# Window attention scores: 64 query rows as they lie in two array halves, no spread copy, blocks written out, the scaling ahead of the next maximum

## The chip, the cores and the metric

The kernel runs on one core of one Trainium2 chip. Its time is the device time of one execution in microseconds (us). The profile is one more execution, recorded by the hardware profiler.

## The reference, cut to what matters

One inference step of a hybrid decoder with two layers, for 1024 prompt tokens and 8 single sample tokens. Each layer projects its input, runs an RWKV-7 time mixing on 8 heads and a sliding-window attention with sinks on 8 query heads (4 to each of 2 key/value heads), then an output projection and a SwiGLU network. The change touches the prompt's attention alone:

```python
def swa_banded(q, k, v, sink):            # T = 1024, BLOCK = WINDOW = 128, HEAD_DIM = 64
    nb = T // BLOCK                       # 8 blocks
    ...
    s = jnp.einsum('bnqkgd,bnskd->bnkgqs', qb, kb).astype(F32) * ATTN_SCALE   # 128 queries x 256 keys
    mask = ((diff >= 0) & (diff < WINDOW))[None] & (kpos >= 0)[:, None, :]
    p = sink_softmax(s, mask, sink[None, None, :, :, None, None])
    o = jnp.einsum('bnkgqs,bnskd->bnqkgd', p.astype(vb.dtype), vb)

def sink_softmax(s, mask, sink):
    s = jnp.where(mask, s, -jnp.inf)
    m = jnp.maximum(jnp.max(s, axis=-1, keepdims=True), sink)
    p = jnp.exp(s - m)
    return p / (jnp.sum(p, axis=-1, keepdims=True) + jnp.exp(sink - m))
```

## The kernel before, in words

Everything lies transposed: 128 rows of features, tokens along the free axis. `proj[:, 15:19]` holds the rotated queries, two heads of 64 rows to a plane, and `kd[:, g]` holds key head g twice, in rows 0 to 63 and in rows 64 to 127. The engines follow programs written by hand, one for each (`block.sync`, `block.gpsimd`, `block.scalar`, `block.vector`, `block.tensor`), and meet by semaphores alone. A layer is a sequence of stages: the input projection, rotation of q and k, the prompt's attention, the sample tokens' attention, the RWKV part, the output projection, the feed-forward part. The stage of the change starts when the last rotated key is there (`kd_last`) and ends when the last block's output has been split (`low`, line 1109); the sample tokens' attention waits for that (line 1724).

In this stage each engine calls its own `blocks(n, q, S, M, V)` for n from -1 to 8. Three parts of three different query blocks stand in one call: S makes the scores of block n+1, M the softmax of block n, V the output of block n-1. The calls for n from 1 to 6 are a hardware loop of three rounds with two calls in each; the others are written out. The parts in one call:

- ScalarE (lines 646 to 686): **bdq**, two copies that put the queries of block n+1 into `q_spread`, where each head's 64 rows have their own 128 columns and the other 64 rows are zero; **vp** and **ptc1**, evictions of transposed values and probabilities; 8 exponentials (`exp0` to `exp7`) that start with a wait for `negmax` of block n, with **ptc3** between the fourth and the fifth; `sinkexp`; `vblk`; **high**, the rounded half of the output of block n-1, which waits for its matmuls `pv`; the scaling of heads 5 to 7.
- VectorE (lines 1061 to 1110): **ptc0**; **sc0** to **sc3**, which take the scores out of banks 0 to 3 with scale and mask, with **ptc2** behind sc0; the **maximum** over 8 heads and three small operations to `negmax` (block n+1); `den` and `recip`, which wait for `sinkexp` (block n); the **scaling** of heads 0 to 4; **low**.
- TensorE (lines 1653 to 1714): `vt`; the transposes **pt0** and **pt1** of the probabilities of block n-1, which wait for both engines' scaling; the scores of the first head pair (**s0**); **pt2** and **pt3**, where pt2 waits for ptc0 and pt3 for ptc1, as they reuse banks 4 and 5; the scores of the other three pairs; the 16 matmuls **pv**, which wait for ptc2 and ptc3.

The scores are computed with all 128 rows, 8 matmuls of 256 columns for a block:

```python
last = mm(bank[p][:, 256 * h:256 * h + 256], bdq[:, p, 128 * h:128 * h + 128],
          kd[:, p // 2, bass.ds((n + 1) * WIN, 2 * WIN)], start=True, stop=True)
```

A float32 matmul stands as two MATMUL records in the trace. sc0 of block n+1 waits for pt3 of block n-1 as well, since both use one score tile.

## Time and profile before

| | |
|---|---|
| three runs, median (lowest to highest) | 3289.95 us (3284.81 to 3290.27) |
| the profiled execution's own time | 3289.88 us |
| its span, first to last instruction | 3287.9 us |
| mean granted TensorE clock | 0.93 |
| busy: TensorE, VectorE, ScalarE, GpSimd | 90%, 45%, 26%, 19% |
| DMA | 158.04 MB, 48 GB/s |

The profile counts from the first instruction. PE is TensorE's matmuls, PEld its weight loads, DVE VectorE, ACT ScalarE. A row of a timeline gives start, length, engine, line, operation, output and inputs, how many of a kind were merged, and in brackets the idle time ahead and who ended it. The stage of the change takes 310.9 to 424.3 in the first layer and about 1935.4 to 2049.1 in the second; the span outside these stretches is some 3060 us.

### The profile page before, as it was taken

What the parts mean: (1) busy time and instruction counts of PE and PEld (TensorE: products, weight loads), DVE (VectorE), ACT (ScalarE), POOL (GpSimd) and SP (SyncE); (2) the same over time, 40 slices, a digit from 0 to 9 for tenths busy, and PEclk for the clock granted to TensorE, in tenths of its full rate; (3) what the DMA queues carried; (4) which work ended last, traced back from release to release, by engine and by line L of the source; (5) the groups of instructions that cost most, each with busy time, mean ns of one, the idle gap of its engine ahead of it and who ended that gap; (6) DMA issues with size and microseconds to landing.
All of it is one profiled execution on the core that took longest, in us unless ns stands there. A gap on an engine that the chain in (4) does not pass through costs nothing.

```text
span 3287.9 us, 49756 instructions
## 1 busy us (share of the span) xinstructions
PE 2954.0 (90%) x20858; PEld 2779.5 (85%) x20858; DVE 1464.9 (45%) x2549; ACT 840.2 (26%) x1759; POOL 609.1 (19%) x297
## 2 busy tenths in 40 slices
PE   6996866997899999999999968579898999999997
PEld 6995745886899999999999947368788999999997
DVE  5335638766632232222363265497646232222324
ACT  3001633341321111111321025424424111111112
POOL 2320001002322212222123100010133212222123
PEclk9998876898999999999999988669899999999998
DMA  3101010003211111111221010100222111111111
GB/s 118 47 32 51 1 39 7 18 19 130 86 46 45 51 41 52 46 46 49 69 71 45 20 52 0 39 11 15 97 80 71 47 45 52 46 45 46 45 52 52
DMA packets 55875, 158.04 MB, mean 48 GB/s; under 512 B 9200, under 2 KB 23536, under 8 KB 54896
## 3 DMA queue, kind: packets, MB, share of 16 engines
q1 hardware_dynamic: 52496, 150.76, 14.2%
q0 software_dynamic: 3168, 4.23, 0.5%
q8 instruction: 162, 2.65, 0.3%
q14 instruction: 49, 0.40, 0.0%
HBM read 137.43 MB, written 17.54 MB: 47 GB/s over the span
## 4 chain that ended last, share of the span: by engine, by line
PE 76%; DVE 13%; issue 5%; ACT 4%; DMA 1%; POOL 0%; SPq 0%; DVEq 0%; ACTq 0%; POOLq 0%
PE bank L1606 20%; PE bank L1608 20%; PE bank L1607 20%; PE bank L1681 2%; PE bank L1713 2%; PE bank L1674 1%; PE bank L1974 1%; PE bank L1970 1%; PE bank L1831 1%; PE bank L1950 1%; PE bank L1773 1%; PE bank L1865 1%; PE bank L1960 1%; DVE c_T L1226 1%; DVE c_NT L1224 1%
## 5 line engine op out<-in xcount | busy, mean ns | idle before, releaser
L1606 PE MATMUL bank<-act_high,w_high 128*128 128x344 f32 x3504 | 1138.1, 325 | 50.8 <-POOL w_low L491 35.6
L1608 PE MATMUL bank<-act_high,w_low 128*128 128x344 f32 x3504 | 1128.5, 322 | 0.0
L1607 PE MATMUL bank<-act_low,w_high 128*128 128x344 f32 x3504 | 1128.2, 322 | 0.0
L491 POOL TENSOR_TENSOR w_low<-w_raw,w_high 128x1024 fp32r<-128x1024 f32 x206 | 521.9, 2539 | 1678.5 <-ACT w_high L580 1661.5
L1606 PEld LDWEIGHTS bank<-act_high,w_high 128*128 128x128 f32 x3504 | 667.8, 191 | 59.6 <-POOL w_low L491 40.4
L1607 PEld LDWEIGHTS bank<-act_low,w_high 128*128 128x128 f32 x3504 | 666.6, 190 | 2.4 <-issue 1.7
L1608 PEld LDWEIGHTS bank<-act_high,w_low 128*128 128x128 f32 x3504 | 667.2, 190 | 0.0
L1469 DVE TENSOR_TENSOR f_mid<-f_silu,bank 128x344 f32<-128x344 f32 x132 | 67.7, 513 | 852.9 <-PE bank L1608 849.7
L1566 DVE TENSOR_TENSOR resid<-bank,resid 128x344 f32<-128x344 f32 x528 | 270.4, 516 | 209.8 <-PE bank L1608 209.8
L1606 PE MATMUL bank<-f_mid_high,w_high 128*128 128x344 f32 x1056 | 341.3, 323 | 4.1 <-DVE resid L1566 4.0
L1608 PE MATMUL bank<-f_mid_high,w_low 128*128 128x344 f32 x1056 | 339.2, 321 | 0.0
L580 ACT CAST w_high<-w_raw 128x1024 fp32r<-128x1024 f32 x206 | 212.5, 1043 | 490.2 <-PE bank L1608 487.1
L1607 PE MATMUL bank<-f_mid_low,w_high 128*128 128x344 f32 x1056 | 337.0, 319 | 0.0
L1606 PEld LDWEIGHTS bank<-f_mid_high,w_high 128*128 128x128 f32 x1056 | 198.1, 188 | 10.7 <-DVE resid L1566 10.1
L1608 PEld LDWEIGHTS bank<-f_mid_high,w_low 128*128 128x128 f32 x1056 | 198.7, 188 | 0.0
L1607 PEld LDWEIGHTS bank<-f_mid_low,w_high 128*128 128x128 f32 x1056 | 198.2, 188 | 0.2
L1023 DVE TENSOR_TENSOR proj<-bank,s_rstd 128x344 f32<-128x344 f32 x126 | 64.3, 516 | 292.1 <-PE bank L1608 292.1
L900 ACT CAST f_mid_high<-f_mid 128x344 fp32r<-128x344 f32 x132 | 63.5, 481 | 406.7 <-DVE f_mid L1469 406.7
L893 ACT ACTIVATE f_silu<-bank 128x344 f32<-128x344 f32 x132 | 60.2, 458 | 351.7 <-PE bank L1608 351.7
L1681 PE MATMUL bank<-a_k_twice,a_q_spread 128*128 (+1 forms) x256 | 71.7, 432 | 15.4 <-ACT a_q_spread L655 14.8
L630 ACT COPY s_raw_last<-proj 128x9 f32<-128x9 f32 x30 | 6.0, 200 | 280.3 <-DVE proj L1023 280.3
L1681 PEld LDWEIGHTS bank<-a_k_twice,a_q_spread 128*128 128x128 f32 x256 | 53.0, 217 | 27.1 <-ACT a_q_spread L655 15.5
(289 smaller groups left out, 3084.3 us busy)
## 6 DMA issues: line engine op xcount, KB each, us to landing
w_raw<-wts SPq DMA_DIRECT2D x206, 512.0 KB, 3.6
resid<-x SPq DMA_DIRECT2D x4, 1376.0 KB, 9.1
att_keep<-act_low SPq DMA_DIRECT2D x2, 2064.0 KB, 10.7
act_low<-att_keep POOLq DMA_DIRECT2D x6, 688.0 KB, 6.1
x_keep<-resid SPq DMA_DIRECT2D x3, 1376.0 KB, 6.4
o_y<-resid SPq DMA_DIRECT2D x3, 1376.0 KB, 5.7
resid<-x SPq DMA_DIRECT2D x4, 516.0 KB, 8.4
resid<-x_keep SPq DMA_DIRECT2D x4, 516.0 KB, 7.9
```

Of the source, the lines that this page charges most:

```text
L491: eng.tensor_tensor(wl[s][:, :], raw[s][:, :], wh[s][:, :].bitcast(F32), ALU.subtract).then_inc(w_low, 1)
L580: eng.copy(wh[s][:, :], raw[s][:, :]).then_inc(w_high, 1)
L893: a(sil[:, c, :], bank[c][:, 0:CW], ACT.Silu).then_inc(scalar_steps, e.step(f"ff{i}_sil{j}{c}"))
L900: eng.copy(mh[:, j, cs(c)], midf[:, c, :]).then_inc(scalar_steps, e.step(f"ff{i}_high{j}{c}"))
L1023: tt(proj[:, k, cs(c)], bank[3 * (k % 2) + c][:, 0:CW], rstd[:, c, :], ALU.mult).then_inc(vector_steps, e.step(f"win_ev{k}{c}"))
L1469: tt(midf[:, c, :], sil[:, c, :], bank[3 + c][:, 0:CW], ALU.mult).then_inc(vector_steps, e.step(f"ff{i}_mid{j}{c}"))
L1566: tt(x[:, k, cs(c)], bank[(DOWN_LAST if i == NR - 1 else DOWN)[n % (4 if i == NR - 1 else 2)]][:, 0:CW], x[:, k, cs(c)], ALU.add).then_inc ...
L1606: mm(out, wh[s][:, wcols], act_h, start=start, stop=False)
L1607: mm(out, wh[s][:, wcols], act_l, start=False, stop=False)
L1608: return mm(out, wl[s][:, wcols], act_h, start=False, stop=stop)
L1681: last = mm(bank[p][:, 256 * h:256 * h + 256], bdq[:, p, 128 * h:128 * h + 128], kd[:, p // 2, bass.ds((n + 1) * WIN, 2 * WIN)], start=Tru ...
L1713: last = mm(bank[6][:, 128 * p:128 * p + 128], v, pT[:, 2 * (2 * p + h) + kt, :], start=(h, kt) == (0, 0), stop=(h, kt) == (1, 1))
```

## The change

1. Scores: a matmul takes one head's 64 rows of queries as they lie in `proj`, against the same 64 rows of `kd`. Head 0 of a pair uses rows 0 to 63, head 1 rows 64 to 127, and each half writes into a bank of its own. Four matmuls, two pairs, make one step (`s0`, `s1`); `q_spread`, its two copies by ScalarE, its clearing by GpSimd and the semaphore `scalar_att` are gone.
2. The loop is written out on the three engines.
3. VectorE: the maximum of block n+1 stands behind the scaling of block n.
4. ScalarE: `high` stands behind the scaling.

```diff
-                for v in (kd[:, :, 0:WIN], vp[0], vp[1], bdq):
+                for v in (kd[:, :, 0:WIN], vp[0], vp[1]):
...
-                    if S:
-                        att.begin()
-                        blk = bass.ds((n + 1) * WIN, WIN)
-                        eng.wait_ge(tensor_att, at_block("tensor_att", "s3", l, n))
-                        for h in range(2):
-                            rows = slice(64 * h, 64 * h + 64)
-                            eng.copy(bdq[rows, :, 128 * h:128 * h + 128], proj[rows, 15:19, blk]).then_inc(scalar_att, att.step(f"bdq{h}"))
...
-                    if V:
-                        eng.wait_ge(tensor_val, at_block("tensor_val", "pv", l, n - 1))
-                        eng.copy(hh[:, 4:8, bass.ds((n - 1) * WIN, WIN)], bank[6][:, :].rearrange("p (k t) -> p k t", k=4)
-                                 ).then_inc(scalar_val, val.step("high"))
                     if M:
                         eng.wait_ge(vector_soft, at_block("vector_soft", "recip", l, n))
                         for h in range(5, 8):
                             a(sm[q][:, h, :], sm[q][:, h, :], ACT.Copy, scale=st(6, h, 1)).then_inc(scalar_soft, soft.step("p_last" if h == 7 else None))
+                    if V:
+                        eng.wait_ge(tensor_val, at_block("tensor_val", "pv", l, n - 1))
+                        eng.copy(hh[:, 4:8, slice((n - 1) * WIN, n * WIN)], bank[6][:, :].rearrange("p (k t) -> p k t", k=4)
+                                 ).then_inc(scalar_val, val.step("high"))
...
-                        for p in range(4):
-                            eng.wait_ge(tensor_att, at_block("tensor_att", f"s{p}", l, n + 1))
-                            stt(sm[o][:, 2 * p:2 * p + 2, :], bank[p][:, :].rearrange("p (h t) -> p h t", h=2), SCALE,
-                                bcast(mk, 1, 2), ALU.mult, ALU.add).then_inc(vector_att, att.step(f"sc{p}"))
+                        for b in range(4):
+                            eng.wait_ge(tensor_att, at_block("tensor_att", f"s{b // 2}", l, n + 1))
+                            h = 4 * (b // 2) + b % 2
+                            stt(sm[o][:, h:h + 3:2, :], bank[b][:, :].rearrange("p (h t) -> p h t", h=2), SCALE,
+                                bcast(mk, 1, 2), ALU.mult, ALU.add).then_inc(vector_att, att.step(f"sc{b}"))
...
-                    def scores(p):
-                        eng.wait_ge(vector_att, at_block("vector_att", f"sc{p}", l, n))
-                        for h in range(2):
-                            last = mm(bank[p][:, 256 * h:256 * h + 256], bdq[:, p, 128 * h:128 * h + 128],
-                                      kd[:, p // 2, bass.ds((n + 1) * WIN, 2 * WIN)], start=True, stop=True)
-                        last.then_inc(tensor_att, att.step(f"s{p}"))
+                    def scores(g):
+                        for h in range(2):
+                            eng.wait_ge(vector_att, at_block("vector_att", f"sc{2 * g + h}", l, n))
+                        for p in range(2):
+                            for h in range(2):
+                                last = mm(bank[2 * g + h][:, 256 * p:256 * p + 256], proj[HEAD[h], 15 + 2 * g + p, slice((n + 1) * WIN, (n + 2) * WIN)],
+                                          kd[HEAD[h], g, slice((n + 1) * WIN, (n + 3) * WIN)], start=True, stop=True)
+                        last.then_inc(tensor_att, att.step(f"s{g}"))
...
-                with eng.Fori(0, NBLK // 2 - 1) as i:
-                    for q in range(2):
-                        blocks(i * 2 + (1 + q), 1 - q, S=True, M=True, V=True)
+                for n in range(1, NBLK - 1):
+                    blocks(n, n % 2, S=True, M=True, V=True)
```

The lines that go from the maximum to `negmax` move unchanged, behind the scaling. VectorE in the call for n = 0, before: four evictions of scores (`a_scores_odd`, block 1), then the maximum and the three small operations, then `den`, `recip` and the scaling of block 0 (`a_scores`).

```order
L1080 SCALAR_TENSOR_TENSOR a_scores_odd<-bank,a_amask 128x512 [waits tensor_scores] x4
L1087 TENSOR_REDUCE a_stats<-a_scores_odd 128x8 [waits vector_scores]
L1089 TENSOR_TENSOR a_stats<-a_stats,params 128x8 [waits vector_scores]
L1091 TENSOR_TENSOR a_stats<-params,a_stats 128x8 [waits vector_scores]
L1092 TENSOR_SCALAR a_stats<-a_stats 128x8
L1100 TENSOR_TENSOR a_stats<-a_stats 128x8 [waits scalar_softmax]
L1102 RECIPROCAL a_stats<-a_stats 128x8 [waits vector_softmax]
L1105 TENSOR_SCALAR a_scores<-a_scores,a_stats 128x256 [waits vector_softmax]
L1105 TENSOR_SCALAR a_scores<-a_scores,a_stats 128x256 x4
```

The same place in the change:

```order
L1071 SCALAR_TENSOR_TENSOR a_scores_odd<-bank,a_amask 128x2x256 [waits tensor_scores] x4
L1083 TENSOR_TENSOR a_stats<-a_stats 128x8 [waits scalar_softmax]
L1085 RECIPROCAL a_stats<-a_stats 128x8 [waits vector_softmax]
L1088 TENSOR_SCALAR a_scores<-a_scores,a_stats 128x256 [waits vector_softmax]
L1088 TENSOR_SCALAR a_scores<-a_scores,a_stats 128x256 x4
L1092 TENSOR_REDUCE a_stats<-a_scores_odd 128x8 [waits vector_scores]
L1094 TENSOR_TENSOR a_stats<-a_stats,params 128x8 [waits vector_scores]
L1096 TENSOR_TENSOR a_stats<-params,a_stats 128x8 [waits vector_scores]
L1097 TENSOR_SCALAR a_stats<-a_stats 128x8
```

The four operations of the next maximum now stand behind the wait for ScalarE's exponentials (`scalar_softmax`) and behind the scaling.

ScalarE at the start of the stage, before: the last copies of keys and values for the cache, the spread copies of blocks 0 and 1, and the load of the table for the exponential with no wait of its own.

```order
L641 COPY a_v_window<-proj 128x8
L655 COPY a_q_spread<-proj 64x4x128 [waits tensor_scores,vector_steps,pool_steps]
L655 COPY a_q_spread<-proj 64x4x128
L655 COPY a_q_spread<-proj 64x4x128 [waits tensor_scores]
L655 COPY a_q_spread<-proj 64x4x128
L667 ACT_TABLE_LOAD
L667 ACTIVATE a_scores,a_stats<-a_scores,a_stats 128x256 [waits vector_scores]
```

The same place in the change:

```order
L639 COPY a_v_window<-proj 128x8
L658 ACT_TABLE_LOAD [waits vector_scores,vector_steps]
L658 ACTIVATE a_scores,a_stats<-a_scores,a_stats 128x256 [waits pool_steps]
L658 ACTIVATE a_scores,a_stats<-a_scores,a_stats 128x256 x3
L664 ACTIVATE a_scores,a_stats<-a_scores,a_stats 128x256 x4
```

The copies are gone, and the table load carries the wait for block 0's `negmax` (`vector_scores`).

TensorE in the call for n = 1, before (two records of the trace to each MATMUL here; ISA and REGISTER_ALU are the loop's register work): pt0, pt1, the scores of one pair, pt2.

```order
L1674 MATMUL bank<-consts,a_scores 128x128 [waits vector_values]
L1674 MATMUL bank<-consts,a_scores 128x128 x3
L1667 REGISTER_ALU
L1674 MATMUL bank<-consts,a_scores 128x128 [waits scalar_values]
L1674 MATMUL bank<-consts,a_scores 128x128 x3
L1694 ISA
L1679 ISA [waits scalar_scores]
L1681 ISA [waits vector_scores]
L1681 MATMUL bank<-a_k_twice,a_q_spread 128x256 x2
L1669 ISA
L1674 MATMUL bank<-consts,a_scores 128x128 [waits vector_values]
L1674 MATMUL bank<-consts,a_scores 128x128 x3
```

The same place in the change, up to the second step of scores:

```order
L1665 MATMUL bank<-consts,a_scores 128x128 [waits vector_values,scalar_softmax,vector_softmax]
L1665 MATMUL bank<-consts,a_scores 128x128 x3
L1665 MATMUL bank<-consts,a_scores 128x128 [waits scalar_values]
L1665 MATMUL bank<-consts,a_scores 128x128 x3
L1674 MATMUL bank<-a_k_twice,proj 128x256 [waits vector_scores]
L1674 MATMUL bank<-a_k_twice,proj 128x256 x3
L1665 MATMUL bank<-consts,a_scores 128x128 [waits vector_values]
L1665 MATMUL bank<-consts,a_scores 128x128 x3
L1665 MATMUL bank<-consts,a_scores 128x128 [waits scalar_values]
L1665 MATMUL bank<-consts,a_scores 128x128 x3
L1674 MATMUL bank<-a_k_twice,proj 128x256 [waits vector_scores]
L1674 MATMUL bank<-a_k_twice,proj 128x256 x3
```

Four matmuls of scores in place of two stand between pt1 and pt2, and the other four follow pt3 in one step.

## Rows read from the trace of the kernel before

**Rows 1.** The page's chain that ended last: shares of the span by engine.

```profile
PE 76%; DVE 13%; issue 5%; ACT 4%; DMA 1%; POOL 0%; SPq 0%; DVEq 0%; ACTq 0%; POOLq 0%
```

**Rows 2.** Stretches: length, busy PE, PEld, DVE, ACT, POOL, granted clock, DMA share, GB/s.

```profile
329.07:415.84 86.77, 70.58 (x439) 63.22 (x440) 56.90 (x118) 58.43 (x188) 0.00 (x0) 0.90 0.00 1
342.12:355.34 13.22, 11.04 (x66) 9.80 (x66) 8.90 (x19) 8.66 (x28) 0.00 (x0) 0.87 0.01 1
355.34:366.75 11.41, 9.36 (x66) 8.43 (x66) 8.78 (x19) 8.39 (x28) 0.00 (x0) 1.00 0.00 0
1953.67:2040.66 86.99, 71.58 (x440) 63.91 (x440) 56.91 (x118) 58.39 (x188) 0.00 (x0) 0.88 0.00 0
```

**Rows 3.** Timeline of VectorE in the call for n = 3.

```profile
356.14 0.69 DVE L1071 COPY a_probs_t<-bank 128x512 f32<-128x512 f32 x1 [0.54 <-PE bank L1674]
...
358.74 0.69 DVE L1080 SCALAR_TENSOR_TENSOR a_scores<-bank,a_amask 128x512 f32<-128x512 f32 x1 [1.91 <-PE bank L1674]
...
361.95 2.29 DVE L1087 TENSOR_REDUCE a_stats<-a_scores 128x8 f32<-128x2048 f32 x1
...
364.63 0.16 DVE L1100 TENSOR_TENSOR a_stats<-a_stats 128x8 f32<-128x8 f32 x1
...
366.39 0.68 DVE L1109 TENSOR_TENSOR act_low<-bank,act_high 128x512 f32 x1
```

**Rows 4.** Timeline of TensorE: calls for n = 3 (355 to 362), n = 2 (345), n = 7 (405, 408).

```profile
345.21 1.92 PE L1674 MATMUL bank<-consts,a_scores_odd 128*128 128x128 f32 x8
...
355.34 1.09 PE L1674 MATMUL bank<-consts,a_scores 128*128 128x128 f32 x8 [1.94 <-ACT a_scores L686]
...
358.44 2.76 PE L1681 MATMUL bank<-a_k_twice,a_q_spread 128*128 x12
361.03 3.73 PE L1713 MATMUL bank<-a_probs_t,a_v_padded 128*128 128x128 f32 x32
...
405.67 1.09 PE L1674 MATMUL bank<-consts,a_scores 128*128 128x128 f32 x8 [0.35 <-DVE a_probs_t L1071]
408.52 5.39 PE L1713 MATMUL bank<-a_probs_t,a_v_padded 128*128 128x128 f32 x32 [1.76 <-ACT a_probs_t L670]
```

**Rows 5.** Timeline of ScalarE in the call for n = 3, and the first copy of n = 4.

```profile
357.15 0.51 ACT L667 ACTIVATE a_scores_odd<-a_scores_odd,a_stats 128x256 f32<-128x256 f32 x1
...
359.13 0.56 ACT L670 COPY a_probs_t<-bank 128x512 f32<-128x512 f32 x1
...
361.58 0.19 ACT L674 ACTIVATE a_stats<-a_stats 128x8 f32<-128x8 f32 x1
...
365.39 1.31 ACT L686 ACTIVATE a_scores_odd<-a_scores_odd,a_stats 128x256 f32<-128x256 f32 x3
366.60 1.25 ACT L655 COPY a_q_spread<-proj 64x512 f32 x2
```

**Rows 6.** Timeline of all engines at the start of the stage.

```profile
310.90 0.63 ACT L637 COPY a_k_tail<-a_k_twice 64x136 f32<-64x136 f32 x2 [73.02 <-DVE a_k_twice L1057]
...
313.07 5.29 PE L1681 MATMUL bank<-a_k_twice,a_q_spread 128*128 128x256 f32 x16 [5.49 <-ACT a_q_spread L655]
...
319.67 1.28 ACT L667 ACT_TABLE_LOAD   x1
...
321.93 0.51 ACT L667 ACTIVATE a_scores<-a_scores,a_stats 128x256 f32<-128x256 f32 x1 [0.98 <-DVE a_stats L1092]
```

**Rows 7.** Timeline of ScalarE: a table load that carries a wait, and its activation.

```profile
459.23 1.28 ACT L724 ACT_TABLE_LOAD   x1 [10.88 <-PE bank L1775]
460.52 1.26 ACT L724 ACTIVATE w_log_decay<-bank,params 128x512 f32<-128x512 f32 x2
```

**Rows 8.** Timeline of TensorE in the RWKV part: matmuls of 64 rows in alternating halves.

```profile
570.72 1.16 PE L1831 MATMUL bank<-ar_heads,bk_heads 64*128 64x128 f32 x16 [0.53 <-ACT proj L764]
571.81 0.43 PE L1881 MATMUL bank<-c_Tt,c_NX 32*32 32x32 f32 x8
...
586.41 2.08 PE L1831 MATMUL bank<-ar_heads,bk_heads 64*128 64x128 f32 x16
```

More of the change, by code:

```diff
@@ L229, in program @@
         kd = sp("k_twice", 2 * (WIN + T))[:, :].rearrange("p (g t) -> p g t", g=2)
-        bdq = sp("q_spread", 4 * 256)[:, :].rearrange("p (k t) -> p k t", k=4)
+        sp("spare", 4 * 256)
         sm = [v[:, :].rearrange("p (h t) -> p h t", h=8) for v in (sp("scores", 8 * 256), at("a_scores_odd", 8 * 256, HH))]
@@ L565, in _ @@
             eng.sem_inc(scalar_steps, CREDIT)
-            eng.sem_inc(scalar_att, CHUNK_CREDIT)
-            att = Chunk(steps, "scalar_att")
             eng.sem_inc(scalar_val, CHUNK_CREDIT)
@@ L1105, in blocks @@
                             ts(sm[q][:, h, :], sm[q][:, h, :], rd[:, h:h + 1], None, ALU.mult).then_inc(vector_soft, soft.step("p_last" if h == 4 else None))
+                    if S:
+                        mine()
+                        mx, nmx, sk = st(0, o), st(2, o), st(4, o)
+                        eng.tensor_reduce(mx, sm[o], AX.X, ALU.max).then_inc(vector_att, att.step())
+                        mine()
+                        tt(mx, mx, sink, ALU.max).then_inc(vector_att, att.step())
+                        mine()
+                        tt(sk, sink, mx, ALU.subtract).then_inc(vector_att, att.step())
+                        ts(nmx, mx, -1.0, None, ALU.mult).then_inc(vector_att, att.step("negmax"))
                     if V:
-                        blk = bass.ds((n - 1) * WIN, WIN)
+                        blk = slice((n - 1) * WIN, n * WIN)
                         eng.wait_ge(scalar_val, at_block("scalar_val", "high", l, n - 1))
@@ L1113, in _ @@
                 blocks(0, 0, S=True, M=True, V=False)
-                with eng.Fori(0, NBLK // 2 - 1) as i:
-                    for q in range(2):
-                        blocks(i * 2 + (1 + q), 1 - q, S=True, M=True, V=True)
+                for n in range(1, NBLK - 1):
+                    blocks(n, n % 2, S=True, M=True, V=True)
                 blocks(NBLK - 1, 1, S=False, M=True, V=True)
@@ L1693, in blocks @@
                     if S:
-                        eng.wait_ge(scalar_att, at_block("scalar_att", "bdq1", l, n + 1))
                         scores(0)
-                        if not V:
-                            scores(1)
                     if V:
@@ L1701, in blocks @@
                     if S:
-                        for p in range(1 if V else 2, 4):
-                            scores(p)
+                        scores(1)
                     if V:
@@ L1718, in _ @@
                 blocks(0, 0, S=True, M=True, V=False)
-                with eng.Fori(0, NBLK // 2 - 1) as i:
-                    for q in range(2):
-                        blocks(i * 2 + (1 + q), 1 - q, S=True, M=True, V=True)
+                for n in range(1, NBLK - 1):
+                    blocks(n, n % 2, S=True, M=True, V=True)
                 blocks(NBLK - 1, 1, S=False, M=True, V=True)
```

14 lines of the change are left out of this document (3 added, 11 removed).

## The prediction, made before the changed kernel ran

> **What bounds the kernel now.** I read the page's chain of work first. TensorE holds 76% of it, VectorE 13%, ScalarE 4% [rows 1]; most of that is the projections and the feed-forward part, which the change leaves alone. So only the stage of the change counts, and inside it I asked who is last. The stretches from the first transposes of block 0 to those of block 7 take 86.77 us in the first layer and 86.99 in the second, for seven calls; TensorE is busy 70.6 of the 86.8, VectorE 56.9, ScalarE 58.4 [rows 2]. None is full: the time is a loop from engine to engine. A call takes 11.41 us where the granted clock is 1.00 (2.4 GHz) and 13.22 where it is 0.87, part of it at 1.2 GHz [rows 2]. The difference, 1.8 us, is TensorE's, so its work lies in the loop.
>
> The timelines show the loop. VectorE: from ptc0 (356.14) to sc0 (358.74) 2.60 us, of which 1.91 idle, waiting for TensorE's transposes; from sc0 to the maximum (361.95) 3.21; from there to `den` (364.63) 2.68; from `den` to `low` (366.39), the scaling, 1.76 [rows 3]. Then the transposes of the next call can start. Between the end of the scaling and sc0 TensorE must do pt0, pt1, one pair of scores, pt2 and pt3, and VectorE has only `low` and ptc0 for that time. At 1.2 GHz the gap widens: eight records of transposes take 1.92 us and not 1.09 [rows 4]. The next maximum, 2.68 us of VectorE's work, is done while nobody but VectorE needs it. The change puts it into this gap.
>
> **The change part by part, first for a call in the middle.** I count from T, the start of ptc0.
> Since pt0, pt1 and the scores of the next block are done under the maximum, only pt2 and pt3 stand between ptc0 and sc0. That case exists in the trace: in the call for n = 7, which makes no scores, pt2 starts 0.35 us after TensorE fell idle, on ptc0's word, and both transposes take 1.09 us [rows 4]. ptc0 takes 0.69 and its release about 0.06, so pt2 starts at T + 0.75, ends with pt3 at 1.84, and sc0 starts at 1.98, against 2.60 now.
> VectorE goes on: four evictions and ptc2 3.21, as now; `den`, `recip` and scaling 1.76; maximum to `negmax` 2.68; `low` 0.60 from its start to the next (its 0.68 less the overlap) [rows 3]. The eviction writes heads h and h+2 and not neighbours, the same 512 elements a row; I take the same 0.69. Sum 1.98 + 3.21 + 1.76 + 2.68 + 0.60 = **10.23 us** at full clock.
>
> Is another engine later? ScalarE starts its exponentials at `negmax`, T - 0.4. From the first to `sinkexp` it takes 4.43 with ptc3 between (357.15 to 361.58) [rows 5], but ptc3 now waits for pt3 (T + 1.84): four exponentials are through at about T + 1.6, so this costs 0.3, and `sinkexp` is written at about T + 4.6. VectorE asks for it at T + 5.19. Slack 0.6: the loop `negmax`, exponentials, scaling, maximum is closed now, at 9.6 us, just under VectorE's own. The bdq copies, 1.25 us of ScalarE a call [rows 5], are gone; they were hidden behind pt0 in part and gave nothing by themselves in this place.
> TensorE: s1 ends at T + 3.0, before sc2 wants it (3.85); pv waits for ptc2 and starts at 3.4, takes 3.73 [rows 4], ends at 7.15, `vt` at 7.3; the scaling ends at 7.0, ScalarE's share (1.31 from `recip` [rows 5]) too; pt0 and pt1 end at 8.4, s0 at 9.5. The next pt2 comes at T + 10.98. So TensorE has 1.4 us of slack, and `high`, now behind the scaling, at 7.9, is there for `low` at 9.6.
>
> What do the array halves give? Scores now: 12 records in 2.76 us, 0.23 each [rows 4]. The nearest row is the RWKV part's line 1831, which alternates halves and banks in the same way: 16 records of 128 columns in 1.16 us, 0.06 each once the last one's own length is off, where pv, of 128 columns too but with all 128 rows, needs 0.11 (32 records in 3.73) [rows 4, 8]. The halves overlap. For 256 columns I take 0.12, so a step of eight records costs about 1.2 us with its tail, at 1.2 GHz twice that (2.08 against 1.16 in the row) [rows 8]. TensorE's work falls by 1.8 us a call, in a place with slack. Bounds: nothing gained (1.9 us a step) or half; at full clock s0 ends by T + 10.2 even then, still ahead of 10.98, so the middle of the stage does not care.
>
> A rule of the Trainium skill speaks against the halves: "TensorEngine Tiling (Array Packing)", Key Properties, says that a change of tiling mode drains the engine. There are four such changes in a call. The trace has the case: after line 1831 the next mode starts 0.07 us before the modelled end, where neighbours of one mode overlap by about 0.17 (358.44 plus 2.76 against 361.03) [rows 4, 8]. So a change of mode costs 0.1 us: by the row 0.1 or 0.2 of 10.23 on the path, some 2 us for both layers, by a drain that ended each step in full not much more. The verdict stays.
>
> Low clock: where the two transposes behind ptc0 fall on 1.2 GHz, the call is 0.83 longer (1.92 less 1.09 [rows 4]), 11.1 us. Over the stage the granted clock is 0.90 [rows 2], so a fifth of the time runs at 1.2 GHz; TensorE's work on the path shrinks to 1.1 us of 10, and I let one call in five meet it there: **10.4 us** a call; bounds 10.2 and 11.1.
>
> **The ends of the stage.** Start: the keys are ready at 310.9, but TensorE starts at 313.07, after bdq [rows 6]; now it starts at 311.0, 2.1 earlier. Scores, evictions and maximum took 8.86 to the first exponential (321.93). Now: s0 1.25, four evictions of 0.62 and the maximum 2.8 make 6.6 at full clock, up to 8.5 at 1.2 GHz. But the load of the exponential's table, 1.28 us, stood under the wait before (319.67, then 0.98 idle) [rows 6]; in the new order it carries the wait for `negmax` itself. The RWKV part shows this form: load after the wait, activation 1.29 later [rows 7]. That is added: exponential at 311.0 + 6.9 + 1.3 = 319.2, bounds 318.9 and 320.8.
> The skill's page "ScalarE: Activation LUTs", What ACT_TABLE_LOAD costs, adds a drain of about 1.38 us to each switch of table. By that the time would be some 2.8 us higher for two layers; rows 7 show no such gap, so it isn't in the sum.
> Eight exponentials without ptc3 take 4.0, `den` to the end of scaling 2.0 with releases: first transposes of block 0 at 319.2 + 6.2 = 325.4, against 329.07 now. The maximum of block 1 comes after it: T of n = 1 is 319.2 + 8.6 = 327.8. TensorE has idled long by then, as before, and I put its first call at 1.2 GHz: transposes 1.92, s0 2.1, so pt2 waits for s0 and not for ptc0, and runs slowly: 1.3 us once. T of n = 7: 327.8 + 1.3 + 6 x 10.4 = 391.5. In that call there is no score, `den` waits for `sinkexp` at T + 4.7, scaling ends 1.85 later, transposes of block 7 at T + 6.9 = **398.4**. There `high` waited for pv of 5.39 us [rows 4] and held up ScalarE's scaling; now it stands behind it. Transposes of block 7 before: 415.84 [rows 2]. What follows is unchanged.
> Gain: 415.84 - 398.4 = 17.4 us a layer, of it 3.7 ahead of block 0's transposes and 13.7 behind. The second layer is the first again (86.99 against 86.77 [rows 2]). Two layers: 34.8 us. GpSimd's clearing was long done and gives nothing. All later stages hang on `low` and shift whole: no weight is fetched in this stage.
> The profiled execution took 3289.88 us, the runs' median is 3289.95; 3289.9 - 34.8 = **3255**.
>
> **The rivals.**
> (a) The clock is low at pt2 and pt3 in every call: 11.1 us, T of n = 7 at 396, and the last call longer by 1.6 too: gain 11.7 a layer, **3266**. For it: fewer columns and waits in the middle of each call. Against it: no idle stretch of TensorE is longer than now (1.94 [rows 4], then 1.5). A call with sixteen records of transposes and 1.94 us of idleness was granted 1.00 throughout [rows 2, 4].
> (b) TensorE's own chain becomes the loop. At 1.2 GHz throughout: transposes 1.9 twice, steps of scores 2.3 twice, pv 5.3, vt 0.3, less overlaps: 13.2 us a call. That eats the whole gain of the calls, and the start's too by slower first steps: **3288**, no change.
> (c) The other side: the halves don't overlap at 256 columns, and the clock is low. Two steps of scores then cost 3.7 each, the chain 16 us a call, and the time is 3289.9 + 2 x 16 = **3322**. It decides from 13.4 us a call. Against it: rows 8.
> (d) The gain is given back later, because the granted clock or a transfer falls differently in the following stages, or the evictions of strided heads are slower (0.1 each: 0.4 a call, 5 us in all): **3258 to 3262**. Or all calls run at 10.2 without the slow first one: 3289.9 - 2 x 20 = **3250**.
>
> **How the numbers follow.** Forecast 3255 with its neighbours 3249 to 3259: 0.58. (a) 0.20, (d) slower 0.12, (b) 0.04, (c) 0.03, larger gain below 3249 0.03. The range takes the forecast, (a) and (d): 3248 to 3268. The runs of before spread by 5.5 us, so 0.2% (6.6 us) is about what can be told from no change. Faster: 0.94, same 0.03, slower 0.03.
>
> **What the new profile would show.** Calls of 10.2 to 10.7 us; VectorE's idle time ahead of sc0 down from 1.91 us [rows 3] to about 1.3; no idle time ahead of `den` in the middle calls, or very little; the table load between `negmax` and the first exponential; scores' steps of 1.2 us; first transposes at 325.4. Idle time ahead of `den` would show ScalarE's loop as the bound; idle time ahead of ptc0 or sc2 would show TensorE's. I would be wrong if ptc0 waited for pt0, or if a change of mode cost much more than 0.1 us.

## The result, and the profile after

| | before | changed |
|---|---|---|
| median of four runs each (lowest to highest) | 3287.45 us (3284.81 to 3290.27) | 3248.18 us (3239.71 to 3249.4) |
| ratio of the times | | 0.9875, 95% interval 0.9855 to 0.9895 |
| profiled execution, its own time | 3289.88 us | 3248.73 us |
| mean granted clock | 0.93 | 0.933 |

The change gains 1.25% by the ratio, 41 us (39.3 by the medians); 34.8 were forecast. The median, 3248.18 us, lies at the fast end of the forecast's range and the ratio puts the time beyond it: 0.9875 of 3287.45 is 3246.4 us, where the range ended at 3248. The sign and the mechanism held; the size of a call did not.

First the stretches of the changed kernel, in the columns of [rows 2]: the call for n = 1, five calls in the middle, the last full one; then the same five and the last of the second layer.

```profile
325.93:336.34 10.41, 9.89 (x65) 8.16 (x66) 8.38 (x18) 6.81 (x23) 0.00 (x0) 0.80 0.01 2
336.34:385.80 49.46, 40.07 (x328) 34.11 (x326) 42.83 (x91) 37.83 (x125) 0.00 (x0) 1.00 0.01 1
385.80:396.50 10.70, 7.51 (x52) 7.07 (x50) 5.80 (x14) 7.57 (x25) 0.00 (x0) 0.84 0.00 1
1933.45:1982.91 49.46, 40.07 (x327) 34.10 (x326) 42.83 (x91) 37.84 (x125) 0.00 (x0) 1.00 0.00 1
1982.91:1992.09 9.18, 5.99 (x52) 5.37 (x50) 5.81 (x14) 7.58 (x26) 0.00 (x0) 1.00 0.00 0
```

Five calls take 49.46 us, 9.89 each, the same in both layers, at a granted clock of 1.00. VectorE is now the busiest, 42.8 of 49.5. From the first transposes of block 0 to those of block 7 (325.93 to 396.50, and 1922.75 to 1992.09) it is 70.57 and 69.34 us, against 86.77 and 86.99 [rows 2].

VectorE's timeline of the call for n = 2 answers to [rows 3]: maximum, low, ptc0, sc0, `den`, and the next maximum.

```profile
335.79 2.28 DVE L1092 TENSOR_REDUCE a_stats<-a_scores 128x8 f32<-128x2048 f32 x1
...
338.46 0.68 DVE L1101 TENSOR_TENSOR act_low<-bank,act_high 128x512 fp32r<-128x512 f32 x1
...
339.06 0.68 DVE L1061 COPY a_probs_t<-bank 128x512 f32<-128x512 f32 x1
...
340.93 0.69 DVE L1071 SCALAR_TENSOR_TENSOR a_scores_odd<-bank,a_amask 128x512 f32<-128x512 f32 x1 [1.19 <-PE bank L1665]
...
342.14 1.88 DVE L1071 SCALAR_TENSOR_TENSOR a_scores_odd<-bank,a_amask 128x512 f32<-128x512 f32 x3
343.93 0.16 DVE L1083 TENSOR_TENSOR a_stats<-a_stats 128x8 f32<-128x8 f32 x1
...
345.68 2.28 DVE L1092 TENSOR_REDUCE a_stats<-a_scores_odd 128x8 f32<-128x2048 f32 x1
```

From ptc0 to sc0 1.87 (forecast 1.98), to `den` 3.00 (3.21), to the maximum 1.75 (1.76), to `low` 2.67 (2.68), to ptc0 0.60. The only idle time is the 1.19 ahead of sc0; `den` waits for nothing. TensorE in the same call, with the first transposes of the next:

```profile
336.34 1.04 PE L1665 MATMUL bank<-consts,a_scores_odd 128*128 128x128 f32 x8
...
337.31 1.13 PE L1674 MATMUL bank<-a_k_twice,proj 64*128 64x256 f32 x8
...
339.80 1.10 PE L1665 MATMUL bank<-consts,a_scores_odd 128*128 128x128 f32 x8 [1.36 <-DVE a_probs_t L1061]
...
342.48 3.81 PE L1702 MATMUL bank<-a_probs_t,a_v_padded 128*128 128x128 f32 x32 [0.52 <-DVE a_probs_t L1075]
...
346.24 1.04 PE L1665 MATMUL bank<-consts,a_scores 128*128 128x128 f32 x8
```

A step of eight records of scores takes 1.13 us. TensorE now waits for VectorE, 1.36 us ahead of pt2 and 0.52 ahead of pv, in place of the other way round. The start of the stage (all engines), with the table load where the listing of instructions had put it, under the wait for `negmax`:

```profile
311.72 5.63 PE L1674 MATMUL bank<-a_k_twice,proj 64*128 64x256 f32 x32 [3.58 <-DVE a_k_twice L1047]
...
318.56 1.28 ACT L658 ACT_TABLE_LOAD   x1 [6.15 <-DVE a_stats L1097]
...
319.86 0.51 ACT L658 ACTIVATE a_scores<-a_scores,a_stats 128x256 f32<-128x256 f32 x1
```

### The profile page after: what moved, and what is told of

It is laid out like the page before. It is cut to its first block, busy times and chain, and to the rows that moved or that the text cites. A ratio compares the mean times of both kernels' runs of the same rounds, so it can differ in the third digit from the quotient of the medians.

```text
span 3246.8 us, 49233 instructions
## 1 busy us (share of the span) xinstructions
PE 2916.8 (90%) x20858; PEld 2741.4 (84%) x20858; DVE 1461.5 (45%) x2549; ACT 824.1 (25%) x1727; POOL 606.3 (19%) x295
## 4 chain that ended last, share of the span: by engine, by line
PE 75%; DVE 16%; ACT 4%; issue 3%; DMA 1%; SPq 0%; POOL 0%; DVEq 0%; ACTq 0%
PE bank L1597 21%; PE bank L1599 20%; PE bank L1598 20%; PE bank L1962 1%; PE bank L1958 1%; PE bank L1938 1%; DVE a_stats L1092 1%; PE bank L1819 1%; PE bank L1853 1%; PE bank L1948 1%; PE bank L1761 1%; DVE act_low L964 1%; DVE c_T L1217 1%; PE bank L1665 1%; DVE c_NT L1215 1%
## 5 line engine op out<-in xcount | busy, mean ns | idle before, releaser
L1254 DVE TENSOR_TENSOR c_gram<-bank,consts 128x512 f32<-128x512 f32 x64 | 41.2, 686 | 69.5 <-PE bank L1819 69.2
L1702 PEld LDWEIGHTS bank<-a_probs_t,a_v_padded 128*128 128x128 f32 x512 | 60.0, 196 | 14.6 <-DVE a_probs_t L1075 10.7
```

The lines of the kernel that those rows point to most:

```text
L1254: tt(GM[n % 2][:, h], bank[h][:, :].rearrange("p (k t) -> p k t", k=4), bcast(c_("gram"), 1, 4), ALU.mult).then_inc(vector_steps, e.step(f ...
L1702: last = mm(bank[6][:, 128 * p:128 * p + 128], v, pT[:, 2 * (2 * p + h) + kt, :], start=(h, kt) == (0, 0), stop=(h, kt) == (1, 1))
```

## The experiments

The theory (T): the gain is the order. The maximum fills the time in which VectorE waited for TensorE, and TensorE's shorter scores have slack. The rivals: the halves make the gain (H), or the written-out loops do (W). Every kernel is compared by ratio with runs of the kernel before on its own chip. For the mechanism I use the stage's own calls, since the rest of the program moves by some microseconds from run to run. A call is measured from the first transpose of one block to that of the next; the column gives the mean of the five middle calls of the first layer, or the two kinds of call where they differ.

| kernel | ratio to before, 95% interval | middle calls, first layer |
|---|---|---|
| order alone | 0.9906 (0.9878 to 0.9935) | 10.33 us |
| halves and written out, old order | 0.9941 (0.9925 to 0.9957) | 10.90 and 12.5 |
| change, loops back on two engines | 0.9891 (0.9863 to 0.9919) | 10.21 |
| before, written out | 0.9993 (0.998 to 1.0006) | 11.2 and 12.9 |
| change, one half | one run, 3267.99 us | 10.02, the first of them 9.62 |
| change, no alternation | 0.9899 (0.9882 to 0.9915) | 9.89 |
| change, high first | 0.9901 (0.9884 to 0.9917) | 10.47, one of 11.94 |
| change, scores over all rows | 0.9891 (0.9876 to 0.9907) | 9.89 |
| change, table early | 0.9869 (0.9852 to 0.9885) | 9.89 |
| change, ptc0 ahead of low | 0.9855 (0.9839 to 0.9872) | 9.29 |
| change, both of these | 0.9843 (0.983 to 0.9857) | 9.29 |
| the same, scaling 4 and 4 | 0.9848 (0.9833 to 0.9862) | 9.03 |

**The order alone.** In the kernel before, the eight lines from the maximum to `negmax` are moved behind the scaling, and `high` likewise:

```diff
-                        mine()
-                        mx, nmx, sk = st(0, o), st(2, o), st(4, o)
...
                     if V and not S:
...
                         for h in range(5):
                             ts(sm[q][:, h, :], sm[q][:, h, :], rd[:, h:h + 1], None, ALU.mult).then_inc(vector_soft, soft.step("p_last" if h == 4 else None))
+                    if S:
+                        mine()
+                        mx, nmx, sk = st(0, o), st(2, o), st(4, o)
...
```

> The kernel before with two moves alone: the maximum and negmax of block n+1 behind the scaling of block n on VectorE, and high behind the scaling on ScalarE; spread copies, full-row scores and loops stay. Theory T (the gain is the order: the maximum fills the time in which VectorE waited for TensorE): the calls shrink, but ScalarE's spread copies (1.25 us) now stand between high and the exponentials, so ScalarE closes the loop at about 11.0 us a call; first transposes of block 0 at about 328, those of block 7 at about 405; 3262 to 3272 us. Theory H (the gain comes from the halves, TensorE's scores being 1.8 us shorter): no change, 3285 to 3290. Theory W (the gain comes from the loops written out): no change, 3285 to 3290.

3259.95 us, 30 us of the 41 and more than I had allowed this kernel (21 to 40 us by the ends of its interval). ScalarE in the call for n = 4, and TensorE's wait for it:

```profile
360.93 1.25 ACT L655 COPY a_q_spread<-proj 64x512 f32 x2
...
362.43 1.13 PE L1682 MATMUL bank<-a_k_twice,a_q_spread 128*128 x4 [1.14 <-ACT a_q_spread L655]
...
362.99 0.51 ACT L667 ACTIVATE a_scores<-a_scores,a_stats 128x256 f32<-128x256 f32 x1
```

The spread copies do stand on ScalarE's path, but at 10.33 us a call and not 11: `high` came at 360.45 and the copies at once behind it. In the second layer the middle calls took 10.43. H and W expected nothing here; both fall as the main cause.

**Halves and written-out blocks in the old order.** In the changed kernel the maximum and `high` go back to their old places:

```diff
+                        mine()
+                        mx, nmx, sk = st(0, o), st(2, o), st(4, o)
...
                     if V and not S:
...
-                    if S:
-                        mine()
...
```

> The changed kernel with the old order on VectorE and ScalarE: maximum ahead of the denominators and the scaling, high ahead of the scaling; halves, no spread copy and written-out blocks stay. Theory T: the calls stay at 11.3 to 12.8 us, since four matmuls of scores in halves between pt1 and pt2 take as long as two before; only the start (2.1 us earlier, less 1.3 for the table load) and small things gain: 3278 to 3287 us. Theory H: most of the 41 us stays, 3248 to 3255. Theory W: the same, 3248 to 3255.

3269.52 us, some 19 us faster than before: half of the full gain, more than T gave it. TensorE in two neighbouring calls:

```profile
338.30 1.09 PE L1664 MATMUL bank<-consts,a_scores_odd 128*128 128x128 f32 x8 [2.22 <-DVE a_scores_odd L1096]
339.32 1.14 PE L1673 MATMUL bank<-a_k_twice,proj 64*128 64x256 f32 x8
340.38 1.09 PE L1664 MATMUL bank<-consts,a_scores_odd 128*128 128x128 f32 x8
...
349.20 1.09 PE L1664 MATMUL bank<-consts,a_scores 128*128 128x128 f32 x8 [2.23 <-DVE a_scores L1096]
350.23 2.03 PE L1673 MATMUL bank<-a_k_twice,proj 64*128 64x256 f32 x8
352.19 1.82 PE L1664 MATMUL bank<-consts,a_scores 128*128 128x128 f32 x8
```

At full clock a call takes 10.90 us against 11.41 [rows 2]; some 0.2 of that is the written-out loop (next experiment), the rest I put down to the copies, and no run separates it. The same wait of 2.2 us stands ahead of both calls, but in the second TensorE runs the critical part at half clock, and that call takes 12.53. Some 8 us of this kernel's gain stand ahead of block 0's transposes: from the last keys to them it takes 14.28 and 14.27 us in the two layers, against 18.17 and 18.30 before. The order alone takes only 0.9 off that stretch (17.28 and 17.36). So with these pieces in place the order brings the rest: 3269.5 to 3248.

**The written-out blocks.** Once as the only change to the kernel before, and once undone in the changed kernel, on VectorE and ScalarE:

```diff
-                for n in range(1, NBLK - 1):
-                    blocks(n, n % 2, S=True, M=True, V=True)
+                with eng.Fori(0, NBLK // 2 - 1) as i:
+                    for q in range(2):
+                        blocks(i * 2 + (1 + q), 1 - q, S=True, M=True, V=True)
```

> The kernel before with the three loops written out and nothing else. Theory T: 0 to 0.3 us a call, so 3283 to 3288 us. Theory W: most of the 41 us, 3248 to 3260. Theory H: as T.

> The changed kernel with the loop of three rounds put back on VectorE and ScalarE; TensorE's blocks stay written out, since its 64-row weights need fixed addresses. Theory T: register work between VectorE's operations costs 0.1 to 0.35 us a call, 12 calls: 3249 to 3253 us, calls of 10.0 to 10.25 against 9.89. Theory W: most of the gain goes, 3275 to 3288.

Written out alone: 3284.66 us, a ratio not told from 1. In the old order it spares 0.2 us of a full-clock call (11.2 against 11.41). Undone: 3254.91 us, 0.16% more than the change and above my range of 3249 to 3253; its interval overlaps that of the change, but the calls are plain. Five middle calls and the last one of the kernel with loops:

```profile
336.73:387.80 51.07, 40.06 (x328) 34.08 (x327) 43.57 (x91) 37.91 (x125) 0.00 (x0) 1.00 0.00 1
387.80:399.81 12.01, 8.72 (x51) 8.11 (x50) 5.90 (x14) 7.57 (x25) 0.00 (x0) 0.72 0.00 0
```

51.07 / 5 is 10.21 us a call, 0.32 more than written out; in the second layer it is 10.10, 0.21 more. VectorE's timeline, from ptc0 of one call to `low` at its end, shows where:

```profile
360.19 0.68 DVE L1062 COPY a_probs_t<-bank 128x512 f32<-128x512 f32 x1
362.17 0.69 DVE L1072 SCALAR_TENSOR_TENSOR a_scores_odd<-bank,a_amask 128x512 f32<-128x512 f32 x1 [1.30 <-PE bank L1667]
...
365.17 0.16 DVE L1084 TENSOR_TENSOR a_stats<-a_stats 128x8 f32<-128x8 f32 x1
...
366.92 2.28 DVE L1093 TENSOR_REDUCE a_stats<-a_scores_odd 128x8 f32<-128x2048 f32 x1
...
369.69 0.69 DVE L1102 TENSOR_TENSOR act_low<-bank,act_high 128x512 f32 x1
```

From ptc0 to sc0 it is 1.98 against 1.87 written out, from the maximum to `low` 2.77 against 2.67, with up to 0.09 more ahead of the next ptc0. From sc0 to `den` it is 3.00, as written out. The last full call took 12.01 us in both layers, at a granted clock of 0.72, against 10.70 and 9.18 in the change.

**How the halves overlap.** The order of the four matmuls is changed to two of one half and then two of the other; then both heads are taken from the lower half:

```diff
-                        for p in range(2):
-                            for h in range(2):
+                        for h in range(2):
+                            for p in range(2):
```

> The changed kernel with the four matmuls of a step of scores in another order: both of rows 0 to 63 first, then both of rows 64 to 127, so that neighbours share a half and can't overlap but at one place. Theory T: a step takes 1.7 to 1.9 us in place of 1.13, but TensorE waits 1.36 us ahead of pt2 and 0.52 ahead of pv in every middle call, so calls stay at 9.9 to 10.0 us: 3247 to 3252 us. Theory H (the halves pay for the gain): the 0.7 us of each step come through, calls of 10.6 to 11.3, 3256 to 3266 us.

The steps took 1.14 us, as with alternation (TensorE, call for n = 3 of this kernel):

```profile
351.96 1.14 PE L1674 MATMUL bank<-a_k_twice,proj 64*128 64x256 f32 x8
```

My expectation of 1.7 to 1.9 us was wrong. The time, 3254.42, is above T's range, though its ratio has an interval that reaches the change's; the calls are 9.89, as T says. Then one half alone:

```diff
-                                last = mm(bank[2 * g + h][:, 256 * p:256 * p + 256], proj[HEAD[h], 15 + 2 * g + p, slice((n + 1) * WIN, (n + 2) * WIN)],
-                                          kd[HEAD[h], g, slice((n + 1) * WIN, (n + 3) * WIN)], start=True, stop=True)
+                                last = mm(bank[2 * g + h][:, 256 * p:256 * p + 256], proj[HEAD[0], 15 + 2 * g + p, slice((n + 1) * WIN, (n + 2) * WIN)],
+                                          kd[HEAD[0], g, slice((n + 1) * WIN, (n + 3) * WIN)], start=True, stop=True)
```

> The changed kernel with both heads of a pair taken from rows 0 to 63, in queries and keys, so that no matmul of scores uses the upper half; the scores of every second head are left wrong. The run without alternation showed steps of 1.13 us as well, so overlap of neighbours may not be what halves them. Theory O (matmuls in different halves overlap, by some looking ahead): with one half alone nothing can, and a step takes 1.9 us. Theory K (a float32 matmul of 64 rows takes half the time of one of 128 by itself): 1.13 us still. The kernel's time by both: 3240 to 3255 us, since the steps have slack.

One run, 3267.99 us. TensorE at the start of the stage and in the call for n = 2:

```profile
313.03 13.99 PE L1674 MATMUL bank<-a_k_twice,proj 64*128 64x256 f32 x32 [3.51 <-DVE a_k_twice L1047]
...
352.02 1.99 PE L1674 MATMUL bank<-a_k_twice,proj 64*128 64x256 f32 x8
```

With one half a step takes 1.99 us, so the gain of 64 rows is overlap of the two halves (theory O), and that overlap doesn't need neighbours to alternate. How far apart they may stand was not tried. The middle calls were 10.0 us, so even 0.85 us more in each step cost 0.1. My range for the whole kernel, 3240 to 3255, was wrong: it was slower in another place, told below.

**Scores over all rows.** The halves are dropped, and nothing is put in for them:

```diff
-                                last = mm(bank[2 * g + h][:, 256 * p:256 * p + 256], proj[HEAD[h], 15 + 2 * g + p, slice((n + 1) * WIN, (n + 2) * WIN)],
-                                          kd[HEAD[h], g, slice((n + 1) * WIN, (n + 3) * WIN)], start=True, stop=True)
+                                last = mm(bank[2 * g + h][:, 256 * p:256 * p + 256], proj[:, 15 + 2 * g + p, slice((n + 1) * WIN, (n + 2) * WIN)],
+                                          kd[:, g, slice((n + 1) * WIN, (n + 3) * WIN)], start=True, stop=True)
```

> The changed kernel with matmuls of scores over all 128 rows of queries and keys as they lie, so that a matmul adds up two heads; this leaves the scores wrong, and only the time counts. Steps of scores take 1.9 us in place of 1.13, everything else stays. Theory T: TensorE has 1.36 us of slack ahead of pt2 and 0.52 ahead of pv, 0.8 us more in each of the two places costs 0 to 0.4 us a call: 3247 to 3255 us, most of the gain stays without any halves. Theory H: 0.8 to 1.6 us a call, 3258 to 3268.

3259.31 us, in the upper range of the two that I gave, but on a chip where the kernel before took 3293.24; the calls decide. The start of the stage, then the call for n = 3:

```profile
310.62 9.75 PE L1674 MATMUL bank<-a_k_twice,proj 128*128 128x256 f32 x32 [3.58 <-DVE a_k_twice L1047]
...
350.48 1.89 PE L1674 MATMUL bank<-a_k_twice,proj 128*128 128x256 f32 x8
353.06 1.09 PE L1665 MATMUL bank<-consts,a_scores 128*128 128x128 f32 x8 [0.69 <-DVE a_probs_t L1061]
```

The steps take 1.89, TensorE's wait ahead of pt2 shrinks from 1.36 to 0.69, and the calls stay at 9.89: the slack pays in the middle of the stage, as T says. It doesn't pay at the start, where the first softmax waits for the scores. The 32 records of blocks 0 and 1 took 9.75 us in the first layer, against 5.63 with halves, and from the first scores to block 0's transposes it was 17.90 and 15.29 us in the two layers, against 14.21 and 14.00; the first call took 11.19 and 10.72 against 10.41 and 10.70. That is some 6 us in this pair of profiles; by the ratios, 0.9891 against 0.9875, it is 5, and the intervals overlap. So in the new order the halves' own speed is worth nothing in the middle calls and some 5 us at the start; the rest of their worth is the copies that they make needless.

**high ahead of the scaling.**

```diff
+                    if V:
+                        eng.wait_ge(tensor_val, at_block("tensor_val", "pv", l, n - 1))
...
                     if M:
                         eng.wait_ge(vector_soft, at_block("vector_soft", "recip", l, n))
...
-                    if V:
-                        eng.wait_ge(tensor_val, at_block("tensor_val", "pv", l, n - 1))
...
```

> The changed kernel with high ahead of ScalarE's scaling, as before. Theory T: high waits for pv, so ScalarE's scaling ends some 1.9 us later, and the transposes with the scores behind them lose their 1.36 us of slack: calls of 10.3 to 10.6 us, 3252 to 3258 us. Rival: the place of high doesn't matter, since pv and the scaling end together: 3246 to 3250.

3255.1 us. ScalarE holds its share of the scaling until pv is through, and TensorE shows it ahead of the transposes and not ahead of pt2 (ScalarE, then TensorE, call for n = 4):

```profile
358.02 0.59 ACT L672 CAST act_high<-bank 128x512 fp32r<-128x512 f32 x1 [2.19 <-PE bank L1702]
358.51 1.30 ACT L677 ACTIVATE a_scores_odd<-a_scores_odd,a_stats 128x256 f32<-128x256 f32 x3
...
359.91 1.06 PE L1665 MATMUL bank<-consts,a_scores_odd 128*128 128x128 f32 x8 [1.81 <-issue]
360.90 1.13 PE L1674 MATMUL bank<-a_k_twice,proj 64*128 64x256 f32 x8
361.97 1.09 PE L1665 MATMUL bank<-consts,a_scores_odd 128*128 128x128 f32 x8
```

10.47 us in four of the five middle calls. The place of `high` is worth 0.58 us of a full-clock call; the fifth took 11.94 at a granted clock of 0.86, and the first call 12.70 against 10.41, in the second layer much the same. So with `high` ahead slow calls come back; the two moves belong together.

**The table load, and a better order.** A one-column exponential ahead of the first block; ptc0 of the next call ahead of `low`, counted by a semaphore of its own; both; and both with four heads' scaling on each engine:

```diff
                 eng.wait_ge(vector_steps, e.at("rq_add32"))
+                a(stat[:, 120:121], stat[:, 120:121], ACT.Exp).then_inc(scalar_steps, e.step("exp_table"))
...
                     if V:
                         val.begin()
-                        eng.wait_ge(tensor_val, at_block("tensor_val", "pt0", l, n - 1))
-                        eng.wait_ge(tensor_val, at_block("tensor_val", "pv", l, n - 2))
-                        eng.tensor_copy(pT[:, 0:4, :], bank[4][:, :].rearrange("p (h t) -> p h t", h=4)).then_inc(vector_val, val.step("ptc0"))
...
+                    if M:
+                        pt0.begin()
+                        eng.wait_ge(tensor_val, at_block("tensor_val", "pt0", l, n))
+                        eng.wait_ge(tensor_val, at_block("tensor_val", "pv", l, n - 1))
+                        eng.tensor_copy(pT[:, 0:4, :], bank[4][:, :].rearrange("p (h t) -> p h t", h=4)).then_inc(vector_pt0, pt0.step("ptc0"))
                     if V:
                         blk = slice((n - 1) * WIN, n * WIN)
```

> The changed kernel with one exponential of a single unused column ahead of the first block, so that the table is loaded while TensorE makes the first scores. Theory T: the first real exponential starts 1.3 us earlier in each layer, 2.6 us in all: 3244 to 3247 us; the table load stands at about 312 and the exponential at about 318.6. By the skill's page on ScalarE, which adds a drain, it would be 5.3 us, 3241 to 3244. Rival: something else is late at the same time, 3247 to 3250.

> The changed kernel with ptc0 of the next call ahead of low on VectorE, under a semaphore of its own. Theory T: low (0.6 us) fills half of the 1.2 us in which VectorE waits for pt2 and pt3, and ScalarE's loop then binds at 9.3 to 9.4 us: calls of 9.35, less 0.5 a call, 3240 to 3244 us. Rival: ScalarE's loop is already the bound, or ptc0 waits for pt0: no change, 3246 to 3250.

> The changed kernel with ptc0 ahead of low and the table loaded early. Theory T: calls of 9.29 us as with ptc0 ahead of low alone, and first transposes 1.4 us earlier: 2 x 1.4 below 3239, if the granted clock leaves it: 3235 to 3240 us. Rival (the early start is given back by a lower clock in the first and last calls, as in the run with the table alone): 3238 to 3243.

> As the one before, and ScalarE scales four heads and VectorE four, in place of three and five. Theory T: VectorE saves 0.28 us a call, ScalarE's scaling ends 0.44 later but still 0.1 ahead of the transposes: calls of 9.0 us, 3232 to 3238 us. Rival: ScalarE's loop binds already, and the transposes wait for its longer scaling: calls of 9.3 or more, 3237 to 3243.

With the table early (3247.46 us, just above T's range and no difference that can be told): the load at 311.86 and, in its profile,

```profile
323.96:335.09 11.13, 10.61 (x65) 8.79 (x66) 8.38 (x18) 6.82 (x23) 0.00 (x0) 0.75 0.01 1
335.09:384.54 49.45, 40.07 (x327) 34.08 (x326) 42.83 (x91) 37.84 (x125) 0.00 (x0) 1.00 0.01 1
384.54:396.24 11.70, 8.51 (x52) 7.91 (x51) 5.80 (x14) 7.56 (x25) 0.00 (x0) 0.71 0.00 1
```

From TensorE's first scores to block 0's transposes it takes 12.79 us against 14.21, 1.42 less. The first call (11.13 against 10.41) and the last (11.70 against 10.70) give it back at a lower clock, 0.75 and 0.71 against 0.80 and 0.84. The gain expected from the load is there and is lost again within the stage. Only the first call's share of that comes with the early load in every profile: 11.07 to 11.22 us in the four layers of the two kernels that differ from their partner by the load alone, against 10.41 to 10.74. The last call doesn't: it ran at 1.00 in both layers of the kernel with both pieces, and in the changed kernel itself at 0.84 in one layer and 1.00 in the other.

ptc0 first: 3239.17 us, about 7 below the change by the ratios, whose intervals overlap, and a microsecond under T's range; the calls, 9.29, are as T gave them. ScalarE's loop, which I had taken for the new bound, isn't it. VectorE's wait ahead of sc0 falls from 1.19 to 0.59 (its call for n = 3) and is still its only one in a middle call:

```profile
348.22 0.68 DVE L1106 TENSOR_TENSOR act_low<-bank,act_high 128x512 fp32r<-128x512 f32 x1
...
349.49 0.69 DVE L1071 SCALAR_TENSOR_TENSOR a_scores<-bank,a_amask 128x512 f32<-128x512 f32 x1 [0.59 <-PE bank L1670]
```

Both: 3241.44 us, ratio 0.9843, the lowest here, though not told apart from 0.9855. The time lies in the rival's range, above T's 3235 to 3240, and this chip's kernel before was 4 us slower than that of ptc0 first; so the runs don't decide. The same with four heads' scaling on each engine has calls of 9.03 us, as computed, and the same total (3244.46, ratio 0.9848), above the 3232 to 3238 that T gave it. The 1.3 us that its five middle calls save in a layer are gone before block 0's transposes. Its first scores ran slower, 6.43 us at a granted clock of 0.59 in the first layer, where those of the kernel with three and five took 5.63 at 0.70:

```profile
313.10 6.43 PE L1680 MATMUL bank<-a_k_twice,proj 64*128 64x256 f32 x32 [3.58 <-DVE a_k_twice L1051]
```

From these scores to the transposes it was 14.38 and 14.39 us in the two layers, against 12.85 and 12.64. Some 0.4 of that is ScalarE's longer scaling; why the clock was lower there was not tried.

## Why the prediction fell short

Held: the loop through TensorE as the bound, and its filling by the maximum; ScalarE's loop shorter than VectorE's (no wait at `den`), though the 9.6 us that I gave it was too long, as with ptc0 first calls of 9.29 still don't wait at `den`; the slack of TensorE; the table load under the wait. The start, from the keys to block 0's transposes, shrank from 18.17 to 14.48 us (310.90 to 329.07, and 311.45 to 325.93): 3.7, as forecast.

Of the four changes of mode in a call, two follow without a wait, and there neighbours overlap by 0.07 us by the modelled ends (336.34 plus 1.04 against 337.31), where pv and `vt`, of one mode, overlap by 0.16 (342.48 plus 3.81 against 346.13). So a change costs the 0.1 us that [rows 8] gave, in a place with slack, and each step still took 1.13. This fits the rule on drains that the Trainium skill gives ("TensorEngine Tiling (Array Packing)", Key Properties), at 0.1 us a change. The table load took 1.28 us and the exponential came 1.30 after its start, so the drain that the Trainium skill's page "ScalarE: Activation LUTs" (What ACT_TABLE_LOAD costs) adds did not show.

**The step that failed** is the sum for a middle call, "1.98 + 3.21 + 1.76 + 2.68 + 0.60 = 10.23", raised to 10.4 for the clock. It measured 9.89 in both layers. Two of its terms and the allowance were too large:
- 0.21 us is "four evictions and ptc2 3.21, as now". From sc0 to `den` it measured 3.00. The 3.21 was read from the old kernel and held two waits that the change takes away. The last eviction waited for the last pair of scores (modelled end 361.19, eviction from 361.24); the last three together took 1.97 us there, and take 1.88 now. Before:

```profile
359.95 1.97 DVE L1080 SCALAR_TENSOR_TENSOR a_scores<-bank,a_amask 128x512 f32<-128x512 f32 x3
```

  And the maximum had to wait for the end of the last eviction, 0.12 us that `den`, now in its place, doesn't need. The kernel with the order alone sheds only this second part: 3.09 us, with its three evictions at 1.97. The loop has no share in this term, since the kernel with the loops back has 3.00 too.
- 0.11 us is the start of sc0 at T + 1.98, which measured 1.87. That part is the loop: with the loops back it is 1.98 again. I had read the release of sc0 from a looped call, register work included, and priced the second part of the change, the writing out, at nothing and without a word.
- 0.17 us was the allowance for half clock. The middle calls ran at 1.00 throughout, in both layers. So did those of all kernels with both moves of the new order, while the five middle calls of the old order got 0.92, written out 0.92 and 0.97, and with halves 0.94; with the maximum moved but `high` ahead it was 0.97. So the order gains twice: by 11.41 to 10.33 at full clock, and by sparing the slow calls.

The total of the kernel with the loops back, 10.21, lies next to my 10.23 by luck. Only 0.11 of its extra time stands in a term that I had too large; the rest stands ahead of `low` and ptc0, where my 2.68 and 0.60 were right for the kernel written out.

Ten middle calls at 0.51 are 5.1 us, most of what was missed: in the profiled executions, between the last keys and the sample tokens' queries, the first layer gained 19.25 us (113.42 to 94.17) and the second 21.1, together 40.4 of the 41.15, where 34.8 were forecast. At the ends I erred in both directions. The call for n = 1, from ptc0 to ptc0, took 10.60 and 10.89 where 11.7 was computed. The last full one, from transposes to transposes, took 10.70 in the first layer, with pv at half clock (5.43 us), and 9.18 in the second; some 10 was computed. Behind it 0.6 us was lost a layer, as ptc0 of block 7 now stands behind a later `low`.

Rival (a), a slow clock at pt2 and pt3, didn't come in the middle calls; rival (b) neither. Of rival (d), the strided evictions take 0.69 each, as before, and the stages behind kept the gain. Rival (c) can be priced in part: in the kernel with one half, without overlap and at a granted clock of 0.57, the first call took 16.31 us (16.86 in the second layer), and 16 was computed. But the calls behind it ran at 1.00 and took 10.0, so even without the overlap only one call in a layer was of that kind, and the time was 3268 and not 3322.

## What to carry to other kernels

When an engine in a loop waits for another, look for its own work that nobody waits for yet and put it into the wait; here that order was worth 30 of 41 us alone, while halving the matmuls' time was worth nothing where they had slack, and some 5 us at the start of the stage, where they had none. A stretch copied from the old timeline holds the old waits: ask of each whether it is still there (0.21 us of each call here). Durations read between operations of a hardware loop hold the loop's register work; where a change writes a loop out, price that (0.2 to 0.3 us a call here). And follow the wait that an instruction ahead of the first use inherits: the table load moved under a wait because a copy ahead of it was removed.

## What the runs showed of the hardware that I had not expected

- Matmuls in the two halves of the array overlap also when two of one half are issued ahead of two of the other: 1.14 us for eight records of 256 columns, 1.99 with one half alone, 1.89 with all 128 rows.
- The granted clock can stay at 1.2 GHz while TensorE is busy. In the kernel with one half the first stretch and the next call were

```profile
313.00:331.80 18.80, 14.47 (x34) 10.68 (x34) 9.60 (x20) 7.74 (x27) 0.00 (x0) 0.50 0.17 63
331.80:348.11 16.31, 16.31 (x65) 13.24 (x66) 9.95 (x18) 6.81 (x23) 0.00 (x0) 0.57 0.00 1
```

  14 us of scores back to back from 313.03 on ran at 0.50. With both halves in use the same 32 records took 5.63 us at 0.70, and with all 128 rows 9.75 at 0.73. Both layers of this one run showed it (12.41 us for the second layer's 32 records, in a stretch at 0.55); why the clock stayed low was not tried.
- A gain ahead of TensorE's work can be taken back in part by its clock: of the 1.4 us that the early table load saved at the start of a layer, the first call gave back 0.5 to 0.7 in all four layers profiled, at a granted clock of 0.72 to 0.75 against 0.78 to 0.80.
